# GpSimd's share of the expert dots goes to VectorE, and the steps around the dots are reordered

## The reference

```python
s = einsum('bthpd,hpnd->bthpn', (h @ w_q), sub_keys)   # 8 heads, 2 halves, 128 keys each
s1, i1 = top_k(s[..., 0], 16);  s2, i2 = top_k(s[..., 1], 16)
top_s, pos = top_k(s1[:, None] + s2[None, :], 16)      # of the 256 sums
expert = (i1 * 128 + i2) at pos;  gate = softmax(top_s)
act = gelu(einsum('cd,ced->ce', h, u[expert]))         # 128 rows of u for each token
y = einsum('ce,ced->cd', gate * act, v[expert])        # 128 rows of v for each token
```

## Time and profile before

| | us |
|---|---|
| median of 2 runs | 2447.26 (2446.34 to 2448.17) |
| profiled execution, its own time | 2435.47 |
| its span | 2433.7 |

### The profile page before, as it was taken

How to read it: one execution, slowest core, us unless ns; L and a number is a source line. 1 busy time by engine, 2 the same in 40 slices (tenths; PEclk the granted TensorE clock), 3 DMA queues, 4 the chain that set the end, 5 groups by cost and what they waited for, 6 DMA issues and landing times. The chain is left out here.

```text
span 2433.7 us, 15718 instructions
## 1 busy us (share of the span) xinstructions
PE 1788.6 (73%) x4869; PEld 866.5 (36%) x4869; DVE 1458.1 (60%) x2431; ACT 496.3 (20%) x1069; POOL 775.4 (32%) x729
## 2 busy tenths in 40 slices
PE   6999999999996655667572344344343599999998
PEld 3444544444444333222231122121111264444443
DVE  5786576241247898474646756565655496555654
ACT  3111121222114345111212112122112171000000
POOL 3312211000004443343333434433543423444441
PEclk9999999999995555998796566666666699999999
DMA  9999799659887666999796666666775799999998
GB/s 345 367 388 384 285 345 375 240 206 350 295 294 300 247 234 239 397 387 374 273 378 270 262 265 259 270 247 261 288 300 209 290 320 370 387 398 393 395 400 338
DMA packets 183663, 768.09 MB, mean 316 GB/s; under 512 B 19584, under 2 KB 26080, under 8 KB 141468
## 3 DMA queue, kind: packets, MB, share of 16 engines
q0 software_dynamic: 92160, 503.36, 53.0%
q1 hardware_dynamic: 89524, 262.87, 29.6%
q10 hardware_dynamic: 1896, 0.86, 0.1%
HBM read 764.89 MB, written 2.13 MB: 315 GB/s over the span
## 5 line engine op out<-in xcount | busy, mean ns | idle before, releaser
L2331 DVE CUSTOM_DVE_ANT_0 arena<-arena,PS 128x2048 f32<-128x2048 f32 x203 | 460.0, 2284 | 179.0 <-DMA arena<-in_peer_u_dram,arena 174.4
L659 POOL DMA_INDIRECT arena<-in_peer_u_dram,arena x256 | 258.5, 1010 | 902.0 <-DVE arena L2233 380.0
L1741 PE MATMUL PS<-arena 128*128 128x512 f32 x256 | 207.1, 956 | 352.7 <-DMA arena<-in_peer_v_dram,causal 345.8
L1750 PE MATMUL PS<-arena 128*128 128x512 f32 x1024 | 445.6, 593 | 3.1 <-DMA arena<-in_peer_v_dram 3.1
L1642 PE MATMUL PS<-arena 128*128 128x512 f32 x688 | 325.4, 622 | 83.6 <-DMA arena<-in_w_out_dram 31.4
L1186 PE MATMUL PS<-arena 128*128 128x512 f32 x720 | 319.5, 594 | 1.4 <-ACT arena L768 1.4
L1750 PEld LDWEIGHTS PS<-arena 128*128 128x128 f32 x1024 | 192.5, 190 | 239.0 <-issue 229.9
L2374 DVE SCALAR_TENSOR_TENSOR PS<-arena,mod_rows_sb,PS 128x1024 f32<-128x1024 f32 x127 | 163.7, 1289 | 117.5 <-DMA arena<-in_peer_v_dram,mod_rows_sb 116.8
L1741 PEld LDWEIGHTS PS<-arena 128*128 128x128 f32 x256 | 65.1, 280 | 457.4 <-DMA arena<-in_peer_v_dram,causal 398.6
L1642 PEld LDWEIGHTS PS<-arena 128*128 128x128 f32 x688 | 129.3, 196 | 268.4 <-issue 149.2
L1186 PEld LDWEIGHTS PS<-arena 128*128 128x128 f32 x720 | 133.2, 190 | 149.8 <-issue 144.4
(11 more groups left out here) (303 smaller groups left out, 1766.7 us busy)
## 6 DMA issues: line engine op xcount, KB each, us to landing
arena<-in_peer_v_dram SPq DMA_DIRECT2D x152, 512.0 KB
arena<-in_ada_w_dram POOLq DMA_DIRECT2D x64, 1024.0 KB, 8.1
arena<-in_w_in_dram SPq DMA_DIRECT2D x112, 512.0 KB, 9.5
arena<-in_ada_w_dram POOLq DMA_DIRECT2D x64, 512.0 KB, 12.0
arena<-in_w_out_dram SPq DMA_DIRECT2D x64, 512.0 KB, 5.9
arena<-in_peer_w_q_dram SPq DMA_DIRECT2D x64, 512.0 KB, 5.5
arena<-in_w_branch_nsa_dram SPq DMA_DIRECT2D x32, 512.0 KB, 6.8
arena<-in_w_branch_mla_dram SPq DMA_DIRECT2D x32, 512.0 KB, 7.2
```

The costliest lines, as they stand in the source:

```text
L659: pool.indirect_dma_start(dst, None, tab, bass.IndirectOffsetOnAxis(ap=idx, axis=0)).then_inc(landed, 16)
L1741: ins = nc.tensor.matmul(PS[:, 2 + k, :], diag[n % 4], Vrow0[n % VRING][:, k * NC:(k + 1) * NC], start=(n == 0), stop=(n == V0_ROWS - 1), ...
L1750: ins = nc.tensor.matmul(PS[:, 4 * t + k, :], A_T[t][:, j, :], Vblk[n % DRING][:, k * NC:(k + 1) * NC], start=(j == NB * t), stop=(j == (N ...
L2331: v.tensor_tensor_reduce(row, row, h, 1.0, 0.0, ALU.mult, ALU.add, dots[:, e:e + 1]).then_inc(u_free, 1)
```

## The change

The products on POOL and the sums on ACT are taken out, so that DVE makes all 256 dots, and it reads `h2` from SBUF in all of them; ACT's copies of `h2` to PSUM are taken out. In `topk_parts` the gates become a part of their own, and the indices come in slot 4 of a head instead of slot 10 (`TOPK_AT`), for the second tile behind a round's first four dots instead of its last. DVE applies the gates a batch later in the slots. The first half row follows u row 140 instead of 136, PE takes a half row three rounds of `a_rows` later and ACT makes its diagonal two batches later. The constant `V0RING` has the value that `VRING` had, 4. The parts that matter:

```diff
-        TOPK_AT, GEXP_AT = (1, 4, 7, 10), 8
+        TOPK_AT, LATE_AT, GEXP_AT = (0, 1, 2, 4, 9), (2, 3, 4, 6, 10), 6
-        POOL_ROWS = tuple(range(20, ROWS, 5)) + tuple(range(ROWS + 4, 2 * ROWS - 8, 8))
@@ POOL: u_row
-                elif i - RING in POOL_ROWS:
-                    pool.wait_ge(u_summed, pool_rows(i - RING + 1))
                 else:
-                    pool.wait_ge(u_free, dve_rows(i - RING + 1))
+                    pool.wait_ge(u_free, i - RING + 1)
@@ POOL
-            def u_product(i):
-                pool.wait_ge(u_in[i % RING], 16 * (i // RING + 1))
-                pool.wait_ge(h2_ready[i // ROWS], 1)
-                row = Urow[i % RING]
-                pool.tensor_tensor(row, row, h2[i // ROWS], ALU.mult).then_inc(u_times, 1)
...
             for i in range(2 * ROWS):
                 u_row(i)
-                if i - RING + 1 in POOL_ROWS:
-                    u_product(i - RING + 1)
-                if i >= ROWS + RING and i % 2 == 0:
-                    v0_row((i - ROWS - RING) // 2)
+                if i >= ROWS + RING + 4 and i % 2 == 0:
+                    v0_row((i - ROWS - RING - 4) // 2)
@@ ACT
-            def row_summed(i):
-                act.wait_ge(u_times, pool_rows(i + 1))
-                row, e = Urow[i % RING], i % TOPK
-                nc.scalar.activation(row, row, ACT.Copy, accum_out=dots[:, e:e + 1]).then_inc(u_summed, 1)
-
-            def h2_across(t):
-                act.wait_ge(h2_ready[t], 1)
-                nc.scalar.copy(PS[:, 4 * t:4 * t + 4, :].rearrange("p a b -> p (a b)"), h2[t]).then_inc(h2ps_ready, 1)
@@ ACT: slots
+                if s == 12:
+                    act.wait_ge(sc_out, 4)
+                if s % TOPK == 12 and u < PH - 2:
+                    act.wait_ge(idx_ready, u + 2)
+                    fetch(scores[0][:, u + 2, :])
...
-                if s - 2 in POOL_ROWS:
-                    row_summed(s - 2)
@@ ACT: rounds of the second tile
                 for b in range(TOPK // BATCH):
                     nb = (PH + r) * 4 + b
                     dots_activated(nb - 1)
+                    if b == 1 and r + 2 < PH:
+                        act.wait_ge(idx_ready, r + PH + 2)
+                        fetch(scores[1][:, r + 2, :])
+                    if b == 1 and r + 1 < PH:
+                        gate_exp(r + PH + 1)
...
-                    for n in range(2):
-                        v0_diag(2 * (nb - PH * 4) + n)
...
-                    for i in range(nb * BATCH, (nb + 1) * BATCH):
-                        if i in POOL_ROWS:
-                            row_summed(i)
+                    for n in range(2 * (nb - PH * 4 - 2), 2 * (nb - PH * 4 - 1)):
+                        if n >= 0:
+                            v0_diag(n)
@@ PE
             for m in range(32):
                 if m:
                     a_rows(m - 1)
-                for n in range(2):
-                    v0_row(2 * m + n)
+                for n in range(2 * (m - 3), 2 * (m - 2)):
+                    if n >= 0:
+                        v0_row(n)
@@ DVE: topk_parts
-                return [lambda: halves(0), lambda: halves(1), candidates, experts]
+                return [lambda: halves(0), lambda: halves(1), candidates, experts, gates_]
@@ DVE: dot
-                if i in POOL_ROWS:
-                    return
...
-                h = h2[0] if i < 16 else PS[:, 4 * t:4 * t + 4, :].rearrange("p a b -> p (a b)")
-                v.tensor_tensor_reduce(row, row, h, 1.0, 0.0, ALU.mult, ALU.add, dots[:, e:e + 1]).then_inc(u_free, 1)
+                v.tensor_tensor_reduce(row, row, h2[t], 1.0, 0.0, ALU.mult, ALU.add, dots[:, e:e + 1]).then_inc(u_free, 1)
@@ DVE: slots
-                if e % BATCH == BATCH - 1 and s >= BATCH:
-                    coefs(s // BATCH - 1)
+                if e % BATCH == BATCH - 1 and s >= 2 * BATCH:
+                    coefs(s // BATCH - 2)
@@ DVE: rounds of the second tile
+            parts = topk_parts(PH + 1)
+            for part in parts[0:2]:
+                part()
             for r in range(PH):
...
-                    if parts:
-                        parts[b]()
-                    coefs(nb - 1)
+                    if b == 0 and parts:
+                        parts[2]()
+                        parts[3]()
+                    if b == 2 and parts:
+                        parts[4]()
+                    if b == 3 and later:
+                        later[0]()
+                        later[1]()
```

More of the change, by code:

```diff
@@ L45 @@
 CD = 1024
-VRING, DRING = 4, 6
+V0RING, VRING, DRING = 4, 4, 6
 WSLOTS = 8
@@ L324, in build @@
         u_in = [sem(f"u_in{i}") for i in range(RING)]
[L325 to L326 removed]
+        v_in = [sem(f"v_in{i}") for i in range(V0RING)]
+        u_free = sem("u_free")
         v_free, d_used = sem("v_free"), sem("d_used")
[L328 removed]
+        gelu_ready, coef_ready, diag_ready = (sem("gelu_ready"), sem("coef_ready"),
                                                           sem("diag_ready"))
@@ L409, in block_landed @@
                          n // DRING + 1)
-        def dve_rows(i):
-            return len([k for k in range(i) if k not in POOL_ROWS])
-        def pool_rows(i):
-            return len([k for k in range(i) if k in POOL_ROWS])
         ROW0 = 2 * KD
@@ L706, in _ @@
                 u_row(i)
-                if i - RING + 1 in POOL_ROWS:
-                    u_product(i - RING + 1)
-                if i >= ROWS + RING and i % 2 == 0:
-                    v0_row((i - ROWS - RING) // 2)
-            for n in range((ROWS - RING) // 2, V0_ROWS):
+                if i >= ROWS + RING + 4 and i % 2 == 0:
+                    v0_row((i - ROWS - RING - 4) // 2)
+            for n in range((ROWS - RING - 4) // 2, V0_ROWS):
                 v0_row(n)
@@ L1099, in _ @@
                 second_projections(s)
-                if s % TOPK == GEXP_AT and u < PH:
+                if s % TOPK == GEXP_AT:
                     gate_exp(u + 1)
@@ L1103, in _ @@
                     dots_activated(b - 1)
-            for i in range(SLOTS - 2, SLOTS):
-                if i in POOL_ROWS:
-                    row_summed(i)
             act.wait_ge(sc_out, 8)
-            h2_across(1)
+            act.wait_ge(idx_ready, PH + 1)
+            fetch(scores[1][:, 1, :])
             def stat_turned(t):
@@ L1165, in _ @@
             a_kept(31)
+            for n in range(2 * 30, V0_ROWS):
+                v0_diag(n)
             stat_turned(1)
@@ L1764, in _ @@
                     a_rows(m - 1)
-                for n in range(2):
-                    v0_row(2 * m + n)
+                for n in range(2 * (m - 3), 2 * (m - 2)):
+                    if n >= 0:
+                        v0_row(n)
             a_rows(31)
+            for n in range(2 * 29, V0_ROWS):
+                v0_row(n)
             turn_stats(1)
@@ L2378, in _ @@
             link(v.tensor_copy(iota_k, iota_i[:, :]))
+            parts = topk_parts(PH + 1)
+            for part in parts[0:2]:
+                part()
             for r in range(PH):
                 u = PH + r
-                parts = topk_parts(u + 1) if r + 1 < PH else []
+                later = topk_parts(u + 2) if r + 2 < PH else []
                 for b in range(TOPK // BATCH):
                     nb = 4 * u + b
-                    for i in range(nb * BATCH, (nb + 1) * BATCH):
-                        dot(i)
-                    if parts:
-                        parts[b]()
-                    coefs(nb - 1)
+                    dot(nb * BATCH)
+                    dot(nb * BATCH + 1)
                     if nb == 4 * PH:
+                        coefs(nb - 1)
                         dve.wait_ge(coef_ready, 4 * PH)
                         v_ready(0)
+                    dot(nb * BATCH + 2)
+                    dot(nb * BATCH + 3)
+                    if b == 0 and parts:
[6 more added lines that the diff above has]
+                        later[1]()
+                    if nb == 4 * PH:
                         dve.wait_ge(stat_out, 1)
+                    else:
+                        coefs(nb - 1)
                     hots(nb - 4 * PH)
+                parts = later
             coefs(8 * PH - 1)
```

63 lines of the change are left out of this document (21 added, 42 removed).

## The result

The changed kernel takes 2221.41 us (median of 2 runs, 2216.45 to 2226.38) against 2447.26: a ratio of 0.9077, 95% interval 0.8989 to 0.9166. A second set of four runs gave 2219.56, ratio 0.9099 (0.9068 to 0.913). The forecast was 2264 us. The profiled execution took 2216.45 us; its span is 2214.7 us where that of before is 2433.7.

What follows compares the result with a forecast made beforehand. The prediction took the second tile's dots to be bound by a loop of POOL, ACT and the ring: 2435.5 - 155 - 10 - 20 + 2 = 2252.5 us, plus 11.8 for the median, 2264 us; range 2203 to 2350.

Steps and rivals of the forecast that it cites:

- Removed: the products and sums of 15 rows, with POOL's wait of 188.7 us for them: Second tile's dots: taking products and sums out removes POOL's 188.7 us wait; early indices remove another 101.8 us.
- The late half rows: After the last u row: six half rows follow instead of four, 2 us of loss, at most 8.
- The dots' length: Second tile's dots: 605 us shrink to 450, gain 155; lower bounds 386 us for DMA and 402 for DVE.
- the 430 to 480 us named as a sign: Sign of the forecast holding: time between the second tile's first and last dot.
- Attention and projections: Second tile's attention gains 10 us (bounds 0 and 20), the projections 20 us (bounds 0 and 40).
- the two nearly cancel: Attention: DVE's ten extra dots, 22 us, against 20.6 us that POOL's products cost DVE's small instructions.
- The reads from SBUF: Dots reading h2 from SBUF hold POOL's transfers until a dot's end; nothing charged beyond the 450 us.
- POOL shut out: Rival, chance 0.25: dots in a row leave POOL no gap; second tile's dots 522 us, total 2336 us.
- Part given back: Rival, chance 0.08: masks, ACT, PE and half row become the new loop, 3.2 us a batch, 2366 us.
- the closed loop: Rival, chance 0.03: half rows hold the u rows behind them, batches run in series; slower, 2686 us.
- No effect: Rival, chance 0.04: gathers slow as they crowd, second tile's dots stay at 269 GB/s; about 2420 us.
- Bare work: Rival, chance 0.1: DVE never waits for long in the second tile's dots, 402 + 4 us; total 2200 us.

Runs made afterwards that it cites:

- e11: The kernel before with products and sums taken out and half rows taken later, indices still late: 2297.4 us, ratio 0.9392 to before.
- e4: The changed kernel with the half rows back at their old distance: 2215.4 us, ratio 0.9087 to before.
- e2: The changed kernel with ACT's copy of h2 to PSUM back and dots reading it from row 16 on: 2204.8 us, ratio 0.9026 to before.
- e7: The changed kernel with h2 read from PSUM and the half rows at their old distance: 2199.9 us, ratio 0.9007 to before.
- e8: The changed kernel with one more 128x512 mask per batch on DVE, written to an unread PSUM bank: 2235.8 us, ratio 0.915 to before.
- e3: The changed kernel with the 37 products, their sums and h2 from PSUM put back: 2242.6 us, ratio 0.919 to before.

## Why the prediction came out as it did

**What bounds the stage: right in kind, wrong in the cause of the biggest term.** "This stage is bound by a loop of POOL, ACT and the ring, not by work" held. But the step "Removed: the products and sums of 15 rows, with POOL's wait of 188.7 us for them" gave that wait to the products. The wait for ACT's sum is 15 times about 13 us, while the sum itself takes 1.9 us; the row of ACT's own wait for PE (453.4 us, the largest of its waits) was not read, and PE's 345.8 us for half rows stood in the earlier trace rows without being used. With the products kept, moving the half rows took the wait to 41.5 us. The total came out well because the change opens the loop twice, at the sums and at the half rows; for this step that was luck, and the total doesn't bear it out.

**The late half rows: priced at 2 us of loss, and wrongly alone.** In the kernel before they are worth 124 us; where no sum stands behind them 6 to 12 us (e11) or nothing that shows (e4). In this change, with the products off, they cost what the forecast had as its bound: the last stage got 7.3 us longer where 2 were forecast and 8 was the most, and e4's 498.1 us say that this is them. Of the 237 us between before and e2, no part of the change "has" a share: alone they give 138, 83 and 124 us, which is 345, and put in last some 38, 90 and nothing. The early indices, which the forecast counted at 101.8 us of 290.5, are the part that the others replace least.

**The dots' length: 450 forecast, 417 measured, the mis-sized term.** What was too careful was the 1.5 us of waiting in each batch, 48 us in all; the dots waited 12.1 us for rows, 0.4 us a batch. With eight buffers two resources that are nearly equal come much closer to their bounds than I allowed, and the 430 to 480 us named as a sign were missed too. The bounds were near: the stage's bytes, 382 GB/s for 417 us or 159 MB, need an estimated 379 us at the 420 GB/s of its best windows, and e7, in which no dot waits for a row, takes 404.0 us where the bound was 402. But that agreement is partly luck. DVE's work was 390.6 us, not 402: dots that follow without a wait take 2.21 us each where most of before's had waited and took 2.29, and one head's 16 best of two halves run ahead of the stage. The 14 us of short pauses between DVE's own instructions, which before had too, were in no term. The stage gained 32 us more than forecast, the stages before it 9 more, the last one 5 less, and the median lay 5 us above the profiled execution instead of 11.8: together the 43 us between 2264 and 2221.

**Attention and projections: 30 forecast, 39.1 measured.** L2052, the last of which started at 965.9 us, is L2020 now:

```profile
L2020 DVE TENSOR_SCALAR nmax<-smax x48: 168/169/385, 311.7 to 938.8; 128x2 f32<-128x2 f32 x48
```

No instruction of 4 or 5 us is left on this line, as forecast, and the end of the attention comes 27.1 us earlier where 10 were forecast and 20 was the bound. That "the two nearly cancel" failed: in e1, which takes only the products out, that last start is at 945.8 us, 20 us earlier, although DVE makes eight dots more by then (18 us). So eight products, with what waited behind their sums, cost this DVE-bound stretch some 38 us and not the 20.6 of the one line by which I counted. Nor were they ten: in the trace of before nine products start between 740 and 985 us, eight of them ahead of that last start. From e1 to the change it comes another 7 us earlier, which is no more than profiles of the same order differ by (937.2 us in e8, 946.9 in e4). The other 12 us are the projections' (forecast 20); DVE's waits for gelu there fell from 73.3 us to 22.8:

```profile
DVE arena L2215 <- ACT act_g L991: 22.8, 2, 19.9
```

**The reads from SBUF: mechanism right, price wrong.** Issues that "end about 0.9 us behind the dot", one at the end of every dot: so it is, back to back too, and POOL was not shut out. "I take nothing beyond the 450 for it" holds against 450, but the stage had room to be shorter, and there it cost 11 us, and 15 in the whole. The Trainium skill, "SBUF — State Buffer", section "Who interferes with whom", would have such dots hold no transfer's issue, which it marks as inferred. 1812 ns beside 964 for the same issue, with nothing changed but where `h2` lies, say that for these indirect transfers they do.

**The rivals.** POOL shut out (522 us for the stage) fell: it gets in between two dots that DVE runs without a pause. Part given back (3.2 us in each batch) and the closed loop fell: POOL waits 10.3 us for PE in the whole stage.

```profile
POOL arena L650 <- issue: 49.4, 162, 0.3
POOL arena L650 <- DVE dots L2294: 34.0, 8, 8.2
POOL arena L650 <- PE PS L1706: 10.3, 12, 1.8
```

No effect fell with 382 GB/s. Bare work (2200 us) was nearest, and with `h2` in PSUM it is what the runs give: 2199.9 and 2204.8 us.

## What to carry to other kernels

When an engine waits for another, read what that one waited for before you price the removal; here "POOL waits for ACT's sum" was a wait for a half row, handed on through PE's list and ACT's list, and moving the half rows was worth nearly as much as taking the sums out. Waits that lie in a row on one engine cover each other: taking one away lengthens the next, so parts of a change have no shares of their own, and the remaining stage is priced by its busy engine, with the pauses between its own instructions, and by its bytes. An engine whose share is 0.99 need not be the one that is waited for: ask who waits. Once the loops are open, what is left is small and is found by adding and taking away a known amount of work on the engine that is nearly full.

## What the runs showed of the hardware

- A dot with both operands in SBUF holds an indirect transfer's issue on POOL until the dot's end, even when the next dot follows at once: 1.90 us instead of 0.94, one issue per dot of 2.21 us, and the dots were not slowed. The expectation before was that dots without a pause might leave no gap.
- The same dot with `h2` in PSUM holds nothing and takes as long.
- A DVE instruction on 128 x 16 values met by a product of 128 x 2048 on POOL takes 4.12 us on average instead of 0.16 (e3 and the change), so that a product hidden on POOL was not free for DVE.
- The core's transfers reached 420 GB/s over 20 us, by gathers of 8 KB rows and 4 KB half rows. The change's window, columns as in the earlier trace rows:

```profile
1400.00:1420.00 20.00, 9.22 (x23) 4.79 (x22) 19.10 (x36) 6.75 (x14) 14.44 (x10) 0.72 1.01 420
```

The Trainium skill, "DMA: Bandwidth & Descriptors", section "Bandwidth", gives 425 GB/s for a 16 MB transfer by one core; the trace agrees.
